# A decoder trunk on one core: recurrence tiles four units apart, the first convolution tap on ScalarE, later spreads at the mixer's end, and first operands ahead of their squares

## What is computed

```python
h = rmsnorm(x, norm_pre[0]);  x = x + 0.5 * rmsnorm(swiglu(h, gate0, up0, down0), norm_post[0])
h = rmsnorm(x, norm_pre[1]);  x = x + rmsnorm(mixer(h), norm_post[1])
h = rmsnorm(x, norm_pre[2]);  x = x + 0.5 * rmsnorm(swiglu(h, gate1, up1, down1), norm_post[2])

# mixer: proj = h @ w_in, split into lru_x (512) | lru_gate (512) | q (256) | k (256) | v (512) | out_gate (512) | low rank (16)
# RG-LRU half:  xc = causal_conv(lru_x, width 4) + conv_b
#               r, i = sigmoid(block_diag(xc) + bias);  a = exp(-8 r softplus(-lam));  m = sqrt(1 - a*a)
#               h_t = a_t h_(t-1) + m_t i_t xc_t;       lru_out = rmsnorm(h * gelu(lru_gate))
# GLA half:     gated linear attention, 4 heads, chunks of tokens, per-head rmsnorm, times silu(out_gate)
# out = concat(lru_out, gla_out) @ w_out
```

## Time and profile before

| what | value |
|---|---|
| runs | 2286.19, 2288.94, 2288.86 us; median 2288.86 |
| the profiled execution, its own time | 2287.83 us |
| its span | 2286.0 us |
| mean granted TensorE clock | 0.987 of full speed |
| busy: TensorE | 2238.6 us |
| busy: VectorE, ScalarE, GpSimd | 1371.3, 1193.0, 727.3 us |

### The profile page before, as it was taken

The page is one execution under the profiler, slowest core; times in us unless marked ns, Lnnn a source line. Parts: engine busy times, 40 slices in busy tenths (PEclk is TensorE's granted clock), DMA queues, the critical chain, the costliest instruction groups (busy, mean ns, idle before and its releaser), DMA issues.

```text
span 2286.0 us, 40462 instructions
## 1 busy us (share of the span) xinstructions
PE 2238.6 (98%) x16890; PEld 2199.2 (96%) x16890; DVE 1371.3 (60%) x1787; ACT 1193.0 (52%) x1840; POOL 727.3 (32%) x793
## 2 busy tenths in 40 slices
PE   8999999999999999999999999999999999999998
PEld 8999999899989999999999999999899898999998
DVE  6554756647776466654574557566578655575454
ACT  6534546635676345543454455574366753454443
POOL 4112512515534124421241124133264422252112
PEclk9999999999999999999999999999999999999999
DMA  6555555344544355555555555544354443555553
GB/s 216 159 165 166 165 167 157 120 118 150 160 143 127 116 165 154 167 163 167 160 165 163 167 162 161 167 147 130 110 176 147 133 135 106 178 159 161 165 168 127
DMA packets 102261, 350.62 MB, mean 153 GB/s; under 512 B 11296, under 2 KB 16416, under 8 KB 102080
## 3 DMA queue, kind: packets, MB, share of 16 engines
q1 hardware_dynamic: 100848, 346.76, 49.5%
q10 hardware_dynamic: 1232, 1.27, 0.2%
HBM read 343.12 MB, written 4.87 MB: 152 GB/s over the span
## 4 chain that ended last, share of the span: by engine, by line
PE 87%; DVE 6%; ACT 5%; POOL 1%; issue 1%; DMA 0%; SPq 0%; DVEq 0%; POOLq 0%
PE psD L445 81%; DVE wl L1032 2%; ACT wh L756 1%; DVE hl L1084 1%; PE psM L587 1%; PE psM L563 1%; DVE kf L1220 1%; POOL inv L1467 1%; DVE diag L1046 1%; DVE y L1070 1%; PE psM L647 1%; PE psM L665 1%; PE psM L636 0%; PE psS L451 0%; ACT L981 0%
## 5 line engine op out<-in xcount | busy, mean ns | idle before, releaser
L445 PE MATMUL psD<-hh,wh 128*128 128x288 f32 x3712 | 1117.3, 301 | 17.2 <-DVE wl L1032 12.6
L445 PE MATMUL psD<-hl,wh 128*128 128x288 f32 x3712 | 1103.9, 297 | 0.0
L445 PE MATMUL psD<-hh,wl 128*128 128x288 f32 x3712 | 1100.1, 296 | 0.0
L1032 DVE TENSOR_TENSOR wl<-raw,wh 128x1024 fp32r<-128x1024 f32 (+1 forms) x656 | 821.8, 1253 | 131.9 <-ACT wh L756 131.8
L756 ACT ACTIVATE wh<-raw 128x1024 fp32r<-128x1024 f32 (+1 forms) x656 | 673.1, 1028 | 154.6 <-DMA raw<-in_w_in 57.7
L445 PEld LDWEIGHTS psD<-hh,wh 128*128 128x128 f32 x3712 | 704.8, 190 | 28.0 <-DVE wl L1032 14.7
L445 PEld LDWEIGHTS psD<-hh,wl 128*128 128x128 f32 x3712 | 707.5, 191 | 0.0
L445 PEld LDWEIGHTS psD<-hl,wh 128*128 128x128 f32 x3712 | 706.0, 190 | 0.8
L1682 POOL TENSOR_TENSOR hidl<-hid,hidh 128x288 fp32r<-128x288 f32 x176 | 211.0, 1199 | 966.4 <-ACT hidh L985 966.4
L445 PE MATMUL psD<-hidh,wh 128*128 128x288 f32 x1408 | 417.7, 297 | 0.0
L445 PE MATMUL psD<-hidl,wh 128*128 128x288 f32 x1408 | 415.3, 295 | 0.0
(11 more groups left out here) (193 smaller groups left out, 1465.1 us busy)
## 6 DMA issues: line engine op xcount, KB each, us to landing
raw<-in_w_gu SPq DMA_DIRECT2D x352, 512.0 KB, 3.6
raw<-in_w_d SPq DMA_DIRECT2D x128, 448.0 KB, 3.2
raw<-in_w_in SPq DMA_DIRECT2D x80, 512.0 KB, 3.6
raw<-in_w_d SPq DMA_DIRECT2D x64, 512.0 KB, 3.6
raw<-in_w_out SPq DMA_DIRECT2D x32, 512.0 KB, 3.6
gates<-in_w_ax SPq DMA_DIRECT2D x4, 512.0 KB, 4.9
S<-in_st_gla SPq DMA_DIRECT2D x4, 512.0 KB, 4.5
out_gla_s<-S SPq DMA_DIRECT2D x4, 512.0 KB, 5.2
```

Of the source, the lines that this page charges most:

```text
L445: mm = e.matmul(out, w[:, kt * P:(kt + 1) * P], t[:, kt, :], start=(kt == 0 and part == 0), stop=(kt == KT - 1 and part == 2))
L1032: e.tensor_tensor(wl[u % RING][:, 0:width], raw[u % RING][:, 0:width], wh[u % RING][:, 0:width].bitcast(F32), ALU.subtract).then_inc(lo_re ...
```

## The change

1. `R_PERIOD` goes from 5 to 4 (`R_END` from 22 to 19), and `W_IN_ORDER` is rewritten so that lru tile t is unit 4t. Everything of the recurrence that stood at 5t+j stands at 4t+j; the gelu goes to slot 19, its product to 21, the square to 22.
2. The first tap of the convolution moves from VectorE (L1151, tensor_scalar) to ScalarE (an activation with Identity, scale and bias), in ScalarE's slot 4t, with a new semaphore `tap_ready`. VectorE does the other three taps together in slot 4t+1.
3. At the mixer's end the diagonals on VectorE, the spreads on TensorE and the values are each one slot later.
4. At the start ScalarE makes all eight operands with four squares in between, then `hi(1)`, `hi(2)`, `hi(3)` with the other squares. VectorE makes all eight `hl` first and then `lo(1)`, `lo(2)` and `lo(3)`; `lo` passes over a unit whose turn was already had.

```diff
-W_IN_ORDER = [0, 8, 9, 10, 11, 1, 4, 5, 6, 7, 2, 16, 17, 18, 19, 3, 12, 13, 14, 15]
-R_PERIOD = 5
+W_IN_ORDER = [0, 4, 8, 9, 1, 5, 10, 11, 2, 6, 7, 16, 3, 17, 18, 19, 12, 13, 14, 15]
+R_PERIOD = 4
...
-T_VALUES = T_SUMS + 4
+T_VALUES = T_SUMS + 5
...
-                if slot == T_SUMS + 3:
+                if slot == T_SUMS + 4:
                     spread_one()
                     e.wait_ge(s_ready, 3 * i + 3)
                 for h in range(HEADS):
-                    if slot == T_SUMS + 3 + (h + 1) // 2:
+                    if slot == T_SUMS + 4 + (h + 1) // 2:
                         spread(psM[:, h, 0:T])
...
         def first_norm(g):
-            for m in range(DT):
-                e.wait_ge(x_landed[g][m // 2], 16)
-                operand(0, 0, g, m)
-                square(g, m, x[g][:, m, :])
-                if g:
+            if g == 0:
+                for m in range(DT):
+                    e.wait_ge(x_landed[g][m // 2], 16)
+                    operand(0, 0, g, m)
+                    if m % 2:
+                        square(g, m // 2, x[g][:, m // 2, :])
+                for u in (1, 2, 3):
+                    hi(u)
+                    for m in range(DT // 2 + 2 * u - 2, min(DT, DT // 2 + 2 * u)):
+                        square(g, m, x[g][:, m, :])
...
             for slot in range(R_END + 4):
+                t = slot // R_PERIOD
+                if slot % R_PERIOD == 0 and t < LT:
+                    q = LT * i + t
+                    e.wait_ge(*taken(s.first + R_PERIOD * t))
+                    if q:
+                        e.wait_ge(xc_ready, q)
+                        e.wait_ge(h_ready, q - 1)
+                    e.activation(cv[0][:, :], xlp[:, 0:W], ACT.Identity, scale=col(par, pk + CONVW + t),
+                                 bias=col(par, pk + CONVB + t)).then_inc(tap_ready, 1)
...
         def lo(u):
-            if u < UNITS:
+            if lows[0] == u < UNITS:
+                lows[0] += 1
...
-                if slot % R_PERIOD == 0 and t < LT:
-                    e.wait_ge(*taken(s.first + R_PERIOD * t))
-                    steps.mark(e.tensor_scalar(cv[0][:, :], xlp[:, 0:W], col(par, pk + CONVW + t), col(par, pk + CONVB + t), ALU.mult, ALU.add))
-                    steps.after()
+                if slot % R_PERIOD == 1 and t < LT:
+                    e.wait_ge(tap_ready, q + 1)
...
-                if slot % R_PERIOD == 1 and t < LT:
-                    steps.after(conv)
+                    steps.after()
...
-                if slot == T_SUMS + 2:
+                if slot == T_SUMS + 3:
                     inverse_ready()
                     before = spreads[0]
                     stat_diagonal(0)
                     stat_diagonal(1)
-                if slot == T_SUMS + 3:
+                if slot == T_SUMS + 4:
                     stat_diagonal(2)
                     stat_diagonal(3)
-                if slot == T_SUMS + 4:
+                if slot == T_SUMS + 5:
                     stat_diagonal(4)
...
         for m in range(DT):
             operand_lo(0, 0, 0, m)
-            if m == 5:
-                lo(1)
+        lo(1)
         lo(2)
+        lo(3)
```

More of the change, by code:

```diff
@@ L315, in program @@
     y_stored = sem("y_stored")
+    tap_ready = sem("tap_ready")
     floor_kept, ident_landed = sem("floor_kept"), sem("ident_landed")
@@ L797, in first_norm @@
         def first_norm(g):
-            for m in range(DT):
-                e.wait_ge(x_landed[g][m // 2], 16)
-                operand(0, 0, g, m)
-                square(g, m, x[g][:, m, :])
-                if g:
-                    yield
[L804 to L808, removed]
+            if g == 0:
[8 more added lines that the diff above has]
+                        square(g, m, x[g][:, m, :])
+            else:
+                for m in range(DT):
+                    e.wait_ge(x_landed[g][m // 2], 16)
+                    operand(0, 0, g, m)
+                    square(g, m, x[g][:, m, :])
+                    yield
                 yield
@@ L835, in recurrence @@
             pk = l * NPAR
+            W = XA - CW + 1
             for slot in range(R_END + 4):
+                t = slot // R_PERIOD
[7 more added lines that the diff above has]
+                                 bias=col(par, pk + CONVB + t)).then_inc(tap_ready, 1)
                 t = (slot - 5) // R_PERIOD
@@ L1026, in _ @@
         spread_of = []
+        lows = [0]
         def lo(u):
-            if u < UNITS:
+            if lows[0] == u < UNITS:
+                lows[0] += 1
                 width = depth(u) * P
@@ L1148, in recurrence @@
                 q = LT * i + t
-                if slot % R_PERIOD == 0 and t < LT:
-                    e.wait_ge(*taken(s.first + R_PERIOD * t))
-                    steps.mark(e.tensor_scalar(cv[0][:, :], xlp[:, 0:W], col(par, pk + CONVW + t), col(par, pk + CONVB + t), ALU.mult, ALU.add))
-                    steps.after()
+                if slot % R_PERIOD == 1 and t < LT:
+                    e.wait_ge(tap_ready, q + 1)
                     steps.mark(e.scalar_tensor_tensor(cv[1][:, :], xlp[:, 1:1 + W], col(par, pk + CONVW + LT + t), cv[0][:, :], ALU.mult, ALU.add))
                     steps.after()
-                    conv = steps.mark(e.scalar_tensor_tensor(cv[0][:, :], xlp[:, 2:2 + W], col(par, pk + CONVW + 2 * LT + t), cv[1][:, :],
+                    steps.mark(e.scalar_tensor_tensor(cv[0][:, :], xlp[:, 2:2 + W], col(par, pk + CONVW + 2 * LT + t), cv[1][:, :],
                                                              ALU.mult, ALU.add))
-                if slot % R_PERIOD == 1 and t < LT:
-                    steps.after(conv)
+                    steps.after()
                     w3 = col(par, pk + CONVW + 3 * LT + t)
```

## The result

| | before | changed |
|---|---|---|
| median of 4 runs each, us | 2287.53 (2285.91 to 2288.94) | 2245.62 (2245.48 to 2245.73) |
| profiled execution, us | 2287.83 | 2245.68 |
| its span, us | 2286.0 | 2243.9 |
| TensorE idle, us | 2286.0 - 2238.6 = 47.4 | 2243.9 - 2223.9 = 20.0 |
| mean granted clock | 0.987 | 0.993 |

A forecast was written before the change was run, and what follows sets the result against it. TensorE bounds the kernel, busy 2238.6 of 2286.0 us. 18.8 + 7.3 + 4.5 + 6.9 - 1.5 = 36 us off 2287.8 gives 2251.8, said as 2252; best end 2242, worst end of the first three cases 2270.

The forecast's parts named there:

- The bound: Whole kernel: time can come only from TensorE's 47 us of idle time and from a lowered clock.
- `xc` term: Projections of mixers 1 and 3: 4.5 us of `xc` waits become 3 us in each, +1.5 us.
- Behind the projection, -18.8: After each mixer's projection: fewer ScalarE table loads there remove the waits for keys and `wl`, 18.8 us in four places.
- The hand-over of the tap: Projection: tap, sigmoid, product, `xc` costs nothing in mixers 0 and 2; in 1 and 3 tile 3 about 2 us late.
- The mixer's end, -7.3: End of each mixer: with spreads one slot later the waits for diagonals go, 7.3 us in four places.
- The start, -4.5: First 40 us: operands first saves waits of 1.8 and 1.2 us and 1.6 us of clock, -4.5 us.
- The clock, the mis-sized term: Behind the stalls after projections and at mixer ends: falls of the clock go with the stalls, -6.9 us.
- I take four of six: Of six clock falls of 1.5 to 1.8 us behind stalls, 10.3 us together, four go: -6.9 us.
- The stall did not move into the projection: Rival: in mixers 1 and 3 the stall moves into the projection, returning about 10.6 us idle, 3 clock: 2266 us, chance 0.20.
- the spreads did not stay late: Rival: at the mixer ends the spreads stay late, keeping 7.3 + 3.4 us: 2262 us, chance 0.15.
- not in sixteen tiles: Rival: gate matmuls of all 16 tiles wait on the hand-over chain, costing 46 us against 36: 2298 us, chance 0.05.

The follow-up runs named there:

- no_ffn_silu: Kernel before with the silu of all ffn stages replaced by a plain copy of the gate: 2263.79 us, 25.1 less, ratio 0.9895.
- tiles_only: Kernel before with recurrence tiles four units apart and the new unit order, first tap still on VectorE: 2259.48 us, 29.2 less, ratio 0.9878.
- tap_on_vector: Changed kernel with the first tap back on VectorE: 2242.30 us, 1.8 less than a repeat of the changed kernel.
- states_later: Changed kernel with the sample chunk's state matmuls one slot after its output matmuls: 2238.64 us, 7.0 less than the changed kernel's 2245.62.
- gates_later: Changed kernel with TensorE's gate matmuls of each tile one slot later: 2245.63 us against 2245.62; a second time 2243.25 us.
- start_only: Kernel before with only the start reordered (operands ahead of squares, `hl` ahead of `lo(1)`): 2283.94 us, 4.7 less, ratio 0.9981.
- tiles_tap: Kernel before with tiles four units apart and the first tap on ScalarE: 2258.48 us.

## Why the prediction was right

It said 2252 us, 36 less than before; the change brought 42, at 2245.6, inside the range.

- **The bound.** Right: nothing was won but TensorE's idle time and clock. The idle terms of the sum, 18.8 + 7.3 + about 2.9 of the start - 1.5, make 27.5 us, and 27.4 were measured. That is closer than its terms deserve: measured they are 18.8, 7.1, 1.9 and an `xc` term of -0.3, so one error of 1.0 and one of 1.2 cancel. The next points have them one by one.
- **Behind the projection, -18.8.** Right in place and size: TensorE was idle for 18.9 us in the four stretches and is for none now. The cause is shown for two thirds of it by `no_ffn_silu`. I expected two loads to stay in the stretch of mixer 0, and three did; 16 vanished from the kernel, as worked out. In the new rows a switch still costs its 1.28 us alone: the load at 624.30 ends at 625.58, and the sigmoid `rg` starts at 625.59. The Trainium skill (ScalarE: Activation LUTs, What ACT_TABLE_LOAD costs) with its 2.66 us is not borne out here either. The timeline of the changed kernel (start, duration, instruction, in brackets the idle time before it and its releaser), first the start, then tile 3 of mixer 1:

```profile
24.05 0.37 PE L446 MATMUL psD<-hh,wh 128*128 128x288 f32 x1 [1.23 <-DVE gate L1057]
...
621.93 0.64 ACT L851 ACTIVATE cv<-xlp,par 128x300 f32<-128x300 f32 x1 [1.71 <-DVE xlp L1433]
...
624.30 1.28 ACT L860 ACT_TABLE_LOAD   x1
625.59 0.50 ACT L860 ACTIVATE rg<-psM,par 128x288 f32<-128x288 f32 x1
625.99 0.50 ACT L861 ACTIVATE ig<-psM,par 128x288 f32<-128x288 f32 x1
626.57 1.04 POOL L1577 TENSOR_TENSOR ig<-ig,xc 128x288 f32<-128x288 f32 x1 [2.38 <-ACT ig L861]
627.74 0.90 DVE L1179 SCALAR_TENSOR_TENSOR xc<-xlp,par,cv 128x256 f32<-128x256 f32 x1 [0.78 <-POOL ig L1577]
628.86 2.29 PE L564 MATMUL psM<-xc,gates 128*128 128x288 f32 x4 [2.15 <-DVE xc L1180]
```

- **The hand-over of the tap.** The rows from 621.93 on are the chain I described, link by link: ScalarE waited 1.71 us for VectorE's take, the product follows the sigmoid, VectorE's last tap waited 0.78 us for the product, and TensorE 2.15 us for `xc`. I had `xc` 2 us late for tile 3 of mixers 1 and 3 and just in time for tile 2, and put 3 us on each mixer; tile 3 was 2.1 us late and tile 2 0.3, 4.8 us in all instead of 6. In mixers 0 and 2 it costs nothing, as forecast. The tap itself was mis-sized: 640 ns, not 530. The 0.62 that the prediction worked out by the Trainium skill (ScalarE: Activation LUTs, What ACT_TABLE_LOAD costs) was nearer. But the hand-over is not what makes `xc` late: with the tap on VectorE the wait is 4.3 us in `tiles_only` and 4.0 in `tap_on_vector`, where VectorE works without a pause. VectorE's list in these two projections is enough for the delay, and the edit meant to relieve it brought nothing.
- **The mixer's end, -7.3.** Right: 0.2 us of 7.3 is left, and alone it is worth 9.6 with its clock.
- **The start, -4.5.** 4.7 measured alone, but that is luck: two wrong sizes cancel. Idle time fell by 1.9 us, not 2.9, and 0.7 of the 1.9 is the first unit's wait (2.0 to 1.3 us), which differs between executions of one kernel; new are 0.5 us for `wl` of unit 1 and 0.8 for the squares' sums, which the prediction had just in time. The clock gave 3.4 us, not 1.6. Unit 3 came at 24.05 us, not near 23; it waits 1.23 us for the gate product, as the first row above shows.
- **The clock, the mis-sized term.** I put 6.9 + 1.6 = 8.5 us on it, and it gave 14.0 by the mean clock (29.7 to 15.7). By place: the start lost 3.4 us and now 0 (I had 1.6); the six falls behind stalls lost 10.2 and now 0 (I had four of six); the four runs of small matmuls, which the prediction left as they were, lost 13.6 and now 10.2; and 3.5 us are new, behind the `xc` waits of mixers 1 and 3. These 3.5 are chance at least in part: waits of the same length had no fall behind them in the kernel before and in `states_later`. The step that failed is "I take four of six", together with counting only falls behind stalls. Half of what the clock cost before lay in four stretches where TensorE never stood. Those I had not looked at, as the waits don't name them.
- **The rivals.** The stall did not move into the projection (4.5 to 4.8 us, not 10.6 more), the spreads did not stay late, and TensorE waits for `xc` in tiles 2 and 3 of two mixers, not in sixteen tiles.

## What to carry to other kernels

When two pieces of work with different activation functions alternate on one engine, count the table loads in the stretch where the next engine stalls: here, taking four of nine loads of 1.28 us away ended two thirds of the stall, and moving one piece of work a few units away, which takes six of the nine and the work itself out of the 41 us, ended all 4.8 us. List the loss to the clock by place as well as the waits, for it also falls where the engine is busy throughout, and there a run of small matmuls split by one full unit was worth 5 to 7 us, more than the last visible wait. And look at where a removed wait goes: of 4.8 us `gates_later` moved about half to other waits, the clock took the rest, and the time hardly changed.

## What the runs showed that I had not expected

- The granted clock falls in pieces that cost about 1.7 us, in or just behind runs of small matmuls with TensorE busy throughout (0.83 over 20 us), and not only behind stalls. Behind stalls it falls only sometimes: five kernels kept the four stalls at the mixer ends (`start_only`, `tiles_only`, `tiles_tap`, `no_ffn_silu` and the kernel before), and 11 of these 20 stalls had a fall behind them.
- The start is such a case too: with the old order every one of five profiles lost 1.7 to 3.4 us there, with the new one seven of nine lost nothing and two 1.7. So a part of what the start gained may be chance in any one execution, though the median of 11 runs of `start_only` is 4.7 us lower.
- With the `xc` waits removed, the four runs of small matmuls lost more to the clock (17.0 us against 10.2, and 13.6 against 8.5), in both profiles of that kernel.
